# Attention units cut by key head, weights scaled on TensorE, and a phase table built five blocks earlier

## The reference, cut to what matters

```python
proj = hn @ w_in[i]                       # 1024 -> 2304 columns
u_ssm, z_ssm, q, k, v, z_attn = jnp.split(proj, SPLIT_IDX, axis=-1)
ssm_out  = s5_branch(u_ssm, ...) * silu(z_ssm)
attn_out = swa_branch(q, k, v, sinks) * silu(z_attn)

# swa_branch: 8 query heads of 64, 2 key heads, blocks of 128 queries that see
# the block before and their own; all in f32
scores = einsum('bnqkgd,bnskd->bnkgqs', qb, kb) / 8 + alibi + mask
m = maximum(max(scores), sink)
e = exp(scores - m)
probs = e / (sum(e) + exp(sink - m))
out = einsum('bnkgqs,bnskd->bnqkgd', probs, vb)

# s5_branch: powers of lam_bar = exp(lam * step) over the sequence, whose phase is
# (time * frequency) modulo one turn
```

## Time and profile before

| | |
|---|---|
| median of 3 runs | 3762.87 us (3760.09 to 3763.44) |
| the profiled execution's own time | 3760.09 us |
| its span, first to last instruction | 3758.3 us |
| PE busy | 3549.3 us, 94% |
| DVE busy | 2005.1 us, 53% |
| ACT busy | 1222.4 us, 33% |
| POOL busy | 1584.4 us, 42% |

### The profile page before, as it was taken

One profiled execution on the slowest core, in us unless ns is written; L12 is line 12 of the kernel. 1 busy time (PEld: TensorE's weight loads), 2 busy tenths in 40 slices (PEclk: granted clock), 3 DMA queues, 4 the chain that ended last, 5 costly groups with the idle time before them and its releaser, 6 DMA issues. The chain is left out here.

```text
span 3758.3 us, 61905 instructions
## 1 busy us (share of the span) xinstructions
PE 3549.3 (94%) x25361; PEld 2793.3 (74%) x25361; DVE 2005.1 (53%) x2410; ACT 1222.4 (33%) x1624; POOL 1584.4 (42%) x1150
## 2 busy tenths in 40 slices
PE   8998999999999899998888879999999999999979
PEld 6876788888888567777777757888888887773757
DVE  6885555554243742225766546555542447758452
ACT  4553333331122642324454423333311221231221
POOL 3432387773332133333333313877733322560352
PEclk9999999999999999998989889999999999999999
DMA  2111122224211132320212021222242112111212
GB/s 97 50 48 35 35 88 84 84 82 147 83 52 39 73 136 94 116 96 31 81 42 81 20 85 40 88 84 84 82 148 83 52 39 104 66 45 40 95 39 73
DMA packets 74496, 276.69 MB, mean 74 GB/s; under 512 B 8256, under 2 KB 8640, under 8 KB 73792
## 3 DMA queue, kind: packets, MB, share of 16 engines
q1 hardware_dynamic: 68544, 252.89, 19.5%
q10 hardware_dynamic: 5760, 20.97, 1.4%
HBM read 208.82 MB, written 65.01 MB: 73 GB/s over the span
## 5 line engine op out<-in xcount | busy, mean ns | idle before, releaser
L117 POOL TENSOR_TENSOR gap<-ones 128x1 f32<-128x1 f32 x152 | 43.1, 284 | 1347.8 <-PE ps L150 873.6
L120 POOL TENSOR_TENSOR wlo<-wraw,whi 128x1024 fp32r<-128x1024 f32 (+3 forms) x152 | 395.8, 2604 | 12.7
L150 PE MATMUL ps<-xh,whi 128*128 128x512 f32 x832 | 269.5, 405 | 40.6 <-DVE xl L3572 10.5
L150 PE MATMUL ps<-xl,whi 128*128 128x512 f32 x832 | 264.1, 399 | 0.0
L150 PE MATMUL ps<-xh,wlo 128*128 128x512 f32 x832 | 263.7, 398 | 0.0
L870 DVE TENSOR_TENSOR h<-ps,h 128x1024 f32<-128x1024 f32 (+1 forms) x56 | 68.5, 1224 | 313.0 <-PE ps L399 274.4
L150 PEld LDWEIGHTS ps<-xh,whi 128*128 128x128 f32 x832 | 155.5, 191 | 93.1 <-DVE xl L3572 13.6
L984 POOL TENSOR_TENSOR wlo<-wraw,whi 128x512 fp32r<-128x512 f32 x126 | 166.8, 1341 | 63.6 <-ACT whi L1107 63.6
L150 PEld LDWEIGHTS ps<-xh,wlo 128*128 128x128 f32 x832 | 158.1, 190 | 38.2
L150 PEld LDWEIGHTS ps<-xl,whi 128*128 128x128 f32 x832 | 158.2, 190 | 38.2
L118 POOL TENSOR_SCALAR whi<-wraw 128x1024 fp32r<-128x1024 f32 (+3 forms) x152 | 179.8, 1183 | 0.0
(11 more groups left out here) (621 smaller groups left out, 9459.3 us busy)
## 6 DMA issues: line engine op xcount, KB each, us to landing
wraw<-w_ffn_in SPq DMA_DIRECT2D x88, 512.0 KB, 3.5
ffn_hidden<-sum_of_squares SPq DMA_DIRECT2D x44, 512.0 KB, 2.6
rw_next<-rw_kept SPq DMA_DIRECT2D x40, 512.0 KB, 5.3
wraw<-w_ffn_out SPq DMA_DIRECT2D x32, 512.0 KB, 3.6
ffn_stage<-ffn_hidden SPq DMA_DIRECT2D x30, 512.0 KB, 5.2
rw_kept<-rw_stage SPq DMA_DIRECT2D x24, 512.0 KB, 2.6
rw_kept<-rw_stage ACTq DMA_DIRECT2D x24, 512.0 KB, 2.7
wraw<-w_ple SPq DMA_DIRECT2D x16, 640.0 KB, 3.8
```

Source lines behind the costliest of these rows:

```text
L117: nc.gpsimd.tensor_tensor(g.gap[:, 0:1], g.ones[:, 0:1], g.ones[:, 0:1], ALU.mult)
L120: nc.gpsimd.tensor_tensor(g.wlo[:, s, 0:w], g.wraw[:, s, 0:w], g.whi[:, s, 0:w].bitcast(F32), ALU.subtract).then_inc(g.w_split.sem, 1)
L150: last = nc.tensor.matmul(acc[:, hf, :], w[:, s, c:c + P], x[:, kt, hf * HALF:(hf + 1) * HALF], start=start and kt == 0 and n == 0, stop=s ...
```

## The change

*Units.* A unit now takes the four heads of one key head (u % 2). All four matmuls of `scores(u)` read the same 64 partitions, and all matmuls of `values(u)` write the same 64 partitions of PSUM, one matmul of 128 columns for each head and key block where there was one of 256 columns for two heads. `attended` copies 64 partitions of 512 elements.

*Scaling.* `normalise` no longer multiplies the weights by 1 / sum. It writes four scaled identity matrices (`adiag`, 128x512), and `turned_weights` multiplies the weights by them with `nc.tensor.matmul`, which transposes and scales at once.

*Look-ahead.* `scores(u + 1)` stands directly in front of `turned_weights(u)`; before, it was `scores(u + 2)` in front of `values(u)`. `maximum` and `exponentials` run one unit ahead.

*Phase table.* The nine operations of a tile are cut into three parts of three. Tiles 0 and 1 run beside blocks 3 to 8, tiles 2 and 3 beside blocks 10 to 15. Tiles 0 and 1 use the rows ZA_ + 2 and ZA_ + 3, and `keep(8)` waits for both to be stored.

```diff
-def turn_work(proj):
-    return proj[:, ZS_ + 2, :], proj[:, ZS_ + 3, :]
+def turn_work(proj, q):
+    n = ZA_ + 2 if q < 2 else ZS_ + 2
+    return proj[:, n, :], proj[:, n + 1, :]
@@ SP
             if q == 4:
                 sp.wait_ge(g.h_saved.sem, 16 * KD)
                 sp.dma_start(bias, g.bias_dram).then_inc(g.bias_loaded.sem, 16)
-            if q >= 6:
-                keep_turn(q - 6)
+                keep_turn(0)
             load(k, q, 1)
...
+            if q == 5:
+                keep_turn(1)
+            if q == 7:
+                keep_turn(2)
@@ POOL
-                if 8 <= beside <= 15:
-                    s5_turn(pool, nc, g, t, proj, (beside - 8) // 2, (beside - 8) % 2)
+                if 3 <= beside <= 8:
+                    s5_turn(pool, nc, g, t, proj, (beside - 3) // 3, (beside - 3) % 3)
+                if 10 <= beside <= 15:
+                    s5_turn(pool, nc, g, t, proj, 2 + (beside - 10) // 3, (beside - 10) % 3)
@@ PE, scores
-            for j in (0, 1):
-                for kv in (0, 1):
-                    c0 = j * WIN + (P if n == 0 else 0)
-                    last = nc.tensor.matmul(g.ps[:, 4 + kv, c0:j * WIN + WIN], proj[key_rows[kv], Q_ + 2 * (u % 2) + j, n * P:(n + 1) * P],
-                                            proj[key_rows[kv], KEY_, k0:(n + 1) * P], start=True, stop=True)
+            for j in range(4):
+                c0 = j % 2 * WIN + (P if n == 0 else 0)
+                last = nc.tensor.matmul(g.ps[:, 4 + j // 2, c0:j % 2 * WIN + WIN], proj[rows, Q_ + j, n * P:(n + 1) * P],
+                                        proj[rows, KEY_, k0:(n + 1) * P], start=True, stop=True)
@@ PE, turned_weights
-                        last = nc.tensor.transpose(g.ps[:, 6 + h // 2, (h % 2 * 2 + kb) * P:(h % 2 * 2 + kb + 1) * P],
-                                                   score[:, u % 2, h, kb * P:(kb + 1) * P], g.ident[:])
+                        last = nc.tensor.matmul(g.ps[:, 6 + j // 2, (j % 2 * 2 + kb) * P:(j % 2 * 2 + kb + 1) * P],
+                                                score[:, u % 2, j, kb * P:(kb + 1) * P], adiag[:, j, :], start=True, stop=True)
@@ PE, values
-            for kb in kbs:
-                for kv in (0, 1):
-                    last = nc.tensor.matmul(g.ps[key_rows[kv], 6, 0:2 * P], vtok[:, n - 1 + kb, key_rows[kv]], probT[:, 2 * kv:2 * kv + 2, kb, :],
+            for j in range(4):
+                kbs = (0, 1) if n else (1,)
+                for kb in kbs:
+                    last = nc.tensor.matmul(g.ps[rows, 6, j * P:(j + 1) * P], vtok[:, n - 1 + kb, rows], probT[:, j, kb, :],
                                             start=kb == kbs[0], stop=kb == 1)
@@ DVE, normalise
-            nc.vector.tensor_tensor(score[:, b, :, k0:], score[:, b, :, k0:], rs[:, b, :].rearrange("p (h o) -> p h o", o=1).broadcast_to([P, 4, WIN - k0]),
-                                    ALU.mult).then_inc(g.prob_ready.sem, 1)
+            if u:
+                dve.wait_ge(g.pt_done.sem, B(g.pt_done, u))
+            nc.vector.tensor_tensor(adiag, eye, rs[:, b, :].rearrange("p (h o) -> p h o", o=1).broadcast_to([P, 4, P]), ALU.mult).then_inc(g.prob_ready.sem, 1)
@@ DVE, order of the units
         maximum(0)
         keep(7)
-        maximum(1)
         normalise(0)
         s5_input(dve, nc, g, t, 2)
         for u in range(UNITS):
             if u + 1 < UNITS:
-                normalise(u + 1)
+                maximum(u + 1)
             if u % 2:
                 m = 8 + u // 2
+                if m == 8:
+                    dve.wait_ge(g.turn_kept.sem, B(g.turn_kept, 32))
...
                 keep(m)
-            if u + 2 < UNITS:
-                maximum(u + 2)
+            if u + 1 < UNITS:
+                normalise(u + 1)
             attended(u)
```

More of the change, by code:

```diff
@@ L2700, in b2_in @@
     mx, neg_mx, es, rs = (t.soft[:, n] for n in range(4))
[L2701 removed]
+    score, probT, vtok, adiag, bias = t.score, t.probT, t.vtok, t.diag, t.bias
     sinks = g.vec[:, VCOL["sinks"]:VCOL["sinks"] + NH]
[L2703 removed]
     diag = g.sumsq[:].rearrange("p (j q) -> p j q", j=NT)
@@ L2846, in values, with opened @@
             pe.wait_ge(g.pt_read.sem, B(g.pt_read, u + 1))
-            n = u // 2
-            kbs = (0, 1) if n else (1,)
-            for kb in kbs:
-                for kv in (0, 1):
-                    last = nc.tensor.matmul(g.ps[key_rows[kv], 6, 0:2 * P], vtok[:, n - 1 + kb, key_rows[kv]], probT[:, 2 * kv:2 * kv + 2, kb, :],
+            n, rows = u // 2, half_rows(u)
+            for j in range(4):
+                kbs = (0, 1) if n else (1,)
+                for kb in kbs:
+                    last = nc.tensor.matmul(g.ps[rows, 6, j * P:(j + 1) * P], vtok[:, n - 1 + kb, rows], probT[:, j, kb, :],
                                             start=kb == kbs[0], stop=kb == 1)
             last.then_inc(g.ao_done.sem, 1)
-        def closed(u):
-            if u + 2 < UNITS:
-                scores(u + 2)
-            values(u)
+        def opened(u):
+            if u + 1 < UNITS:
+                scores(u + 1)
+            turned_weights(u)
         def beside(m, kt):
             u = 2 * (m - 8)
-            if m == 7 and kt == 5:
+            if m == 7 and kt == 6:
                 scores(0)
-            if m == 8 and kt == 0:
-                scores(1)
             if m >= 9 and kt == 0 and u - 1 < UNITS:
-                turned_weights(u - 1)
+                opened(u - 1)
             if m >= 9 and kt == 2 and u - 1 < UNITS:
-                closed(u - 1)
+                values(u - 1)
             if m >= 8 and kt == 4 and u < UNITS:
-                turned_weights(u)
+                opened(u)
             if m >= 8 and kt == 6 and u < UNITS:
-                closed(u)
+                values(u)
             if m == NPROJ - 1 and kt == 4:
@@ L2939, in _ @@
             ins.then_inc(g.pt_read.sem, 1)
-            if u + 2 < UNITS:
-                exponentials(u + 2)
+            if u + 1 < UNITS:
+                exponentials(u + 1)
         act.wait_ge(g.acc_free.sem, first + 10)
@@ L2999, in maximum @@
             dve.wait_ge(g.source_read.sem, B(g.source_read, u + 1))
-            nc.vector.tensor_tensor(two(es[:, b, :]), two(sinks)[:, :, 2 * b:2 * b + 2], two(mx[:, b, :]), ALU.subtract)
+            nc.vector.tensor_tensor(es[:, b, :], sinks[:, 4 * kv:4 * kv + 4], mx[:, b, :], ALU.subtract)
             nc.vector.tensor_scalar(neg_mx[:, b, :], mx[:, b, :], -1.0, None, ALU.mult).then_inc(g.shift_ready.sem, 1)
@@ L3234, in s5_turn @@
         link(nc.gpsimd.tensor_scalar(r, r, 1.0, -ROUND, ALU.mult, ALU.add))
+    if part == 1:
         link(nc.gpsimd.tensor_tensor(d, d, r, ALU.subtract))
-    if part == 1:
         link(nc.gpsimd.tensor_tensor(tiles(r), time, rate(t.f2), ALU.mult))
         link(nc.gpsimd.tensor_tensor(d, d, r, ALU.add))
+    if part == 2:
         link(nc.gpsimd.tensor_scalar(r, d, 1.0, ROUND, ALU.mult, ALU.add))
```

26 lines of the change are left out of this document (13 added, 13 removed).

## The result

The changed kernel takes **3821.44 us** (median of four runs, 3819.48 to 3823.35) against 3762.73 us for the kernel before in the same session (four runs, 3760.09 to 3763.44): a ratio of **1.0156**, 95% interval 1.0144 to 1.0169. In a later session it took 3821.42, a ratio of 1.0164 (1.0146 to 1.0182).

A forecast was written before the change was run, and what follows sets the result against it. PE was taken as the bound (130.3 of 133.0 us busy), DVE just below. 3760.1 + 42.3 - 2.7 + 20.9 + 3 = 3823.6, and 2.8 more for the median gave 3826 us; range 3799 to 3843.

The forecast's parts named there:

- PE work of the units: Attention units on PE: longer scores, values and transposing matmuls plus shape changes, 2.82 us per full unit, +42.3 us together.
- changes of tile shape: PE in each attention unit: scores and values no longer touch, so one more shape change, taken as 0.1 us.
- waits of the earlier trace: Transposes of the first units waiting for `attended`: the longer unit gives DVE more time, so -2.7 us.
- clock behind that: PE after its last idle piece before the first unit: six us at half clock lose 3 us (0 to 8).
- The ratio of 0.8: Preparation before the first `normalise`: each us of POOL work delays DVE 0.8 us, 24.0 for 30.0; bounds 0.5 and 1.
- The standstill: PE before block 9, waiting for DVE's late first `normalise`: 20.9 us in all, bounds 11.9 to 26.9.
- The wait of `keep(8)`, SP's queue, the shorter look-ahead: Blocks 8 and 9 and later units: tiles stored in time, block loads early enough, round trip fits one unit; all cost 0.
- DVE absorbs POOL: Rival: POOL's operations cost DVE little more than its margin, so only PE's part stays, 3802 us; chance 13%.
- packing wasn't the reason: Rival: packing didn't make scores and values fast; they cost as before, transposes alone add 14.4 us, 3798; chance 5%.
- Four times faster transposes: Rival: f32 transposes are four times faster than full matmuls, so 25 us more for the units, 3851; chance 4%.
- delay and clock feed each other: Rival before and in the first units: ratio 1 and 8 us of low clock, 3837 to 3845; chance 11%.
- Not slower: Rival: the engines' round trip sets the unit's 8.73 us, so longer PE parts fill gaps, 3760 us; chance 5%.

The follow-up runs named there:

- Units only: The control: the changed kernel with the phase table back at its old place beside blocks 8 to 15; 3802.49 us, ratio 1.0095.
- halves apart: The kernel before, with the second half's two matmuls of `scores` issued one slice (six matmuls of L150) later; 3791.66 us, ratio 1.0071.
- second parts left out: The changed kernel without the second part (three POOL operations each) of phase table tiles 0 and 1; 3814.55 us, ratio 1.0137.
- table only: The kernel before with only the phase table moved and cut in three parts; 3782.97 us, ratio 1.0052.
- scaled identities only: The kernel before with `normalise` writing scaled identities and full matmuls in place of the weights' transposes; 3775.31 us, ratio 1.0033.
- Order of the halves: The kernel before, matmuls of one partition half issued together, then the other's, in `scores` and `values`; 3764.40 us, ratio 0.9999.

## Why the prediction was right

The control splits the 60.75 us. Units only give 39.77. The change is 305.81 - 284.83 = 20.98 us longer than that, with the same PE work. The windows over the whole stage (length, then PE's busy time) show how, first of the change, then of units only:

```profile
3148.03:3453.84 305.81, 290.28 (x1553) 231.00 (x1552) 187.38 (x361) 65.14 (x179) 130.09 (x87) 0.97 0.17 59
3144.99:3429.82 284.83, 284.83 (x1554) 226.88 (x1552) 171.91 (x361) 65.40 (x179) 123.72 (x87) 1.00 0.18 63
```

15.5 us are PE's idle time, and it is busy 5.5 us longer with the same matmuls, nearly all of it by the lower clock. (At each of the five waits 0.16 us of the busy time is the end of a record, as in halves apart; about 4.7 are left for the clock.)

| step | forecast | measured |
|---|---|---|
| PE work of the units | 42.3 | 42.5 (39.77 + 2.7) |
| scores / values, each unit | 0.88 / 0.88 | 0.86 / 0.87 |
| weights, each unit | 0.96 | 0.92 |
| changes of tile shape, each unit | 0.1 | 0.2 |
| unit to unit | 11.55 | 11.58 |
| waits of the earlier trace rows | -2.7 | -2.7 |
| first `normalise` later | 24.0 | 22.9 |
| DVE keeps PE from its first transposes | 20.9 | 18.8 |
| clock behind that | 3 | 2.2 |

- *PE's work* was right to 0.2 us, in part because two small errors cancel. The weights went from 0.79 to 1.71 us with nothing else changed, 0.92 for the 0.96 of the sum. They take 1.81 where scores stand directly in front, 0.10 for a change of tile shape. A second 0.1 stands ahead of the values, where the last pair of L150 takes 0.56 for 0.47. The sum had one of the two. With both, 0.86 + 0.87 + 0.92 + 0.20 = 2.85, which is 11.58 - 8.73.
- *The ratio of 0.8* was a choice between 0.5 and 1. It measured 22.9 / 30.0 = 0.76, in second parts left out 0.74, in table only (23.6 us late) 0.79. Ratio 1 did not come in this mix. The earlier trace rows show why: even an operation that is held for all of POOL's 2.71 us loses only 2.09 by it, 0.77, since its own 0.69 are done in the same time. The 30.0 us are POOL's operations at their undisturbed length, and so are the 3.4 of a split; the split of block 7 in the earlier trace rows took 1.05 + 2.71 = 3.76, as DVE slows POOL too. In the changed kernel the phase operations of that stretch took 33.1 us for 26.6, so for each us that POOL really works DVE loses less than 0.76.
- *The standstill and the clock* came out 2.9 us under the sum together, 21.0 for 23.9. PE came to its first transposes 114.61 us into the stage. That is 19.8 later than the 94.81 of the kernel before, as 22.9 - 3.1 says, but 18.8 later than the 95.80 of the control: the scores ahead of them are 1.0 longer by themselves, and the sum counts this 1.0 twice, in PE's work and in the standstill. The other 1.1 is the ratio. Behind the first transposes 2.2 us are left, the half clock until 3267, for the 3 of the sum. Not all of the 18.8 shows as waiting. After the waits before block 6 PE ran at half clock (0.57 from 3212 to 3220), and the slow matmuls filled part of the time that it would have stood. So the list of waits has only 15.5 us. The sum had put such a covered drop at nothing, and it was right to: it is the same time under another name.
- *The median* of 3826 lies 4.6 above the result. The terms are 63.5 for 60.75, so 2.8 of it are theirs; no term explains the rest, which is less than the runs scatter.
- *The wait of `keep(8)`, SP's queue, the shorter look-ahead* cost nothing, as said: no wait of PE lies behind block 8.

The rivals. That DVE absorbs POOL fell with table only. That packing wasn't the reason fell with halves apart. Four times faster transposes fell with scaled identities only. That delay and clock feed each other stays a size: 4.7 to 5.5 us of clock in all, of which 2.2 aren't covered, of the 8 that it needed, at 0.76. Not slower fell with units only, where PE idles nowhere and the longer records set the pace.

One step was wrong in its words though not in its number: that *neighbours* in opposite halves run side by side. Order of the halves shows that neighbours don't matter; whether the other half has work at all does.

What stays open: how far apart in PE's list two halves may be and still overlap. With the four records of one half directly ahead of the four of the other they overlap; with the values and a slice of full-width matmuls between them they don't. Whether it is the distance or the other tile shape between them that parts them, no run tells.

## What to carry to other kernels

When PE matmuls use half of the rows or columns, count the work of each half: the longer one was the time here, in both orders tried, as long as the two halves stood together in the list. Before filling POOL's idle time, look whether DVE has slack in that stretch: each us of POOL work that reads SBUF made DVE's list here, mostly operations with two SBUF inputs, about 0.75 us longer, so idle POOL can be the cheapest place only where DVE is idle too or reads PSUM. And run the part that nothing disturbs as a control; its stage length split the rest into waits and clock.

## What the runs showed of the hardware

- The overlap of the two halves doesn't need alternation: eight records of 256 columns take 1.07 us in the order A A B B (1.06 in A B A B) and 1.92 us when all are in one half.
- A full f32 matmul of 128x128x128 costs about two f32 transposes: eight take 1.71 us for 0.79.
- POOL memsets next to DVE work with two SBUF inputs cost it nothing (0.68 us, as alone), while a POOL tensor_tensor of the same size made 0.69 into 2.77.
- A DVE copy from SBUF to SBUF with a single input was held too: 2.95 us for two of 128x512, against 0.75.
- POOL is slowed too while DVE works: 3.26 and 3.37 us for a tensor_tensor that takes 2.39.
- Behind idle pieces of 0.74 and 2.03 us, with 1.16 us of scores between them, PE's next matmuls ran at half clock (2.08 us for 1.05); with the same two pieces filled they ran at full clock.
